# A chunked delta-rule layer: where projection units stand between the products of the triangular inversion's levels 1 to 5

## The reference, cut to what matters

```python
proj = x @ w_in
...
    k_beta = k * beta[..., None]
    a_mat = jnp.where(strict, jnp.einsum("bhncd,bhnsd->bhncs", k_beta, k) * decay, 0.0)
    rhs = jnp.concatenate([v * beta[..., None], k_beta * jnp.exp(gc)[..., None]], axis=-1)
    sol = lax.linalg.triangular_solve(a_mat, rhs, left_side=True, lower=True, unit_diagonal=True)
...
    def step(state, xs):
        u_c, w_c, qk_c, qd_c, kd_c, gl_c = xs
        v_new = u_c - jnp.einsum("bhcd,bhdv->bhcv", w_c, state)
        o_c = (jnp.einsum("bhcd,bhdv->bhcv", qd_c, state)
               + jnp.einsum("bhcs,bhsv->bhcv", qk_c, v_new))
        state = state * gl_c[..., None, None] + jnp.einsum("bhcd,bhcv->bhdv", kd_c, v_new)
        return state, o_c
```

## Time and profile before

| | |
|---|---|
| median of 3 runs | 2631.28 us (2630.43 to 2633.28) |
| the profiled execution's own time | 2627.11 us |
| its span, first to last instruction | 2625.5 us |
| PE busy over the span | 2399.2 us (91%) |
| DVE, ACT, POOL busy | 1760.8, 1331.4, 688.8 us |
| mean granted TensorE clock | 0.962 |
| the 16 solves | from about 200 to 1150 us of the span |

### The profile page before, as it was taken

How to read it: one execution, slowest core, us unless ns; L and a number is a source line. 1 busy time by engine, 2 the same in 40 slices (tenths; PEclk the granted TensorE clock), 3 DMA queues, 4 the chain that set the end, 5 groups by cost and what they waited for, 6 DMA issues and landing times. The chain is left out here.

```text
span 2625.5 us, 40683 instructions
## 1 busy us (share of the span) xinstructions
PE 2399.2 (91%) x11739; PEld 1957.8 (75%) x11740; DVE 1760.8 (67%) x2231; ACT 1331.4 (51%) x1735; POOL 688.8 (26%) x674
## 2 busy tenths in 40 slices
PE   7989988989999899967999887799999998999995
PEld 6868777877777788855787665688888887888782
DVE  3347888788778866645864585667767787677645
ACT  3254465456456544433531132567767776667640
POOL 2002121111221111104101222544444443444330
PEclk9989999999999999978999998899999999999997
DMA  3334432322233253335574234789999999899935
GB/s 116 74 45 72 62 49 58 87 65 49 65 65 64 54 91 99 93 112 185 156 232 174 96 97 153 251 276 341 291 289 299 321 327 346 283 285 297 330 78 214
DMA packets 244142, 435.92 MB, mean 166 GB/s; under 512 B 25096, under 2 KB 149000, under 8 KB 244046
## 3 DMA queue, kind: packets, MB, share of 16 engines
q1 hardware_dynamic: 211198, 350.70, 44.2%
q0 software_dynamic: 32848, 83.96, 12.3%
HBM read 370.88 MB, written 97.71 MB: 178 GB/s over the span
## 5 line engine op out<-in xcount | busy, mean ns | idle before, releaser
L59 PE MATMUL dn_pj<-x_hi,dn_hi 128*128 128x512 f32 x1024 | 433.9, 424 | 1.8 <-PEq L84 1.8
L61 PE MATMUL dn_pj<-x_hi,dn_lo 128*128 128x512 f32 x1024 | 406.6, 397 | 0.0
L60 PE MATMUL dn_pj<-x_lo,dn_hi 128*128 128x512 f32 x1024 | 405.0, 396 | 0.0
L1044 DVE SCALAR_TENSOR_TENSOR uc_half<-u_in,par,uc_half 128x512 f32<-128x512 f32 x480 | 378.4, 788 | 13.1
L59 PE MATMUL gu_ps<-e_hi,xg_hi 128*128 (+1 forms) x752 | 311.4, 414 | 0.0
L2520 DVE TENSOR_TENSOR e_lo<-e_raw,e_hi (+1 forms) x128 | 292.5, 2286 | 19.2 <-ACT e_hi L2459 19.0
L61 PE MATMUL gu_ps<-e_hi,xg_lo 128*128 (+1 forms) x752 | 295.7, 393 | 0.0
L60 PE MATMUL gu_ps<-e_lo,xg_hi 128*128 (+1 forms) x752 | 294.6, 392 | 0.0
L2459 ACT ACTIVATE e_hi<-e_raw (+1 forms) x128 | 245.1, 1917 | 42.4 <-PEq L84 35.5
L61 PEld LDWEIGHTS dn_pj<-x_hi,dn_lo 128*128 128x128 f32 x1024 | 195.7, 191 | 44.9
L59 PEld LDWEIGHTS dn_pj<-x_hi,dn_hi 128*128 128x128 f32 x1024 | 196.8, 192 | 33.7 <-issue 2.9
(11 more groups left out here) (388 smaller groups left out, 4966.1 us busy)
## 6 DMA issues: line engine op xcount, KB each, us to landing
e_raw<-in_w_gate_e_dram SPq DMA_DIRECT2D x128, 512.0 KB, 5.9
e_raw<-in_w_up_e_dram SPq DMA_DIRECT2D x128, 512.0 KB, 9.4
e_raw<-in_w_down_e_dram SPq DMA_DIRECT2D x128, 512.0 KB, 8.0
dn_raw<-in_w_in_dram SPq DMA_DIRECT2D x64, 512.0 KB, 7.9
gate_rows<-qkv_next SPq DMA_DIRECT2D x16, 512.0 KB, 3.1
br_raw<-in_w_oa_dram SPq DMA_DIRECT2D x16, 512.0 KB, 4.7
br_gate<-gate_rows SPq DMA_DIRECT2D x32, 256.0 KB, 4.6
br_raw<-in_w_ob_dram SPq DMA_DIRECT2D x16, 512.0 KB, 4.3
```

Of the source, the lines that this page charges most:

```text
L59: nc.tensor.matmul(out, w_hi, x_hi, start=first, stop=False)
L60: nc.tensor.matmul(out, w_hi, x_lo, start=False, stop=False)
L61: return nc.tensor.matmul(out, w_lo, x_hi, start=False, stop=last)
L1044: ins = stt(out=uc[:], in0=u_in[:, t:t + HALF], scalar=w, in1=uc[:], op0=ALU.mult, op1=ALU.add)
```

## The change

In levels 1 to 4 one unit stands behind Y, one behind T and one behind Z, where none, one and two stood before. In group 3, which has four units a level, it is one, one and two, where it was none, two and two. At level 5 the units that stood between T and Z (one, or two in group 3) stand between Y and T, and none is left between T and Z. Level 6 is as it was. The number of units is the same, and no other engine's list changes.

```diff
@@ -692,6 +692,7 @@
                                 last = mm(ga[:, pr, :], ar[l % NA][:, 2 * pr:2 * pr + 2, :].rearrange(FLAT),
                                           left_pair(xx, l, pr), start=True, stop=True)
                             last.then_inc(y_done, 1)
+                            f(1 if l < LEVELS - 2 or more else 2)
                             pe.wait_ge(xr_ready, q * 5 + l)
                             for pr in range(2):
                                 last = tr(gc[:, pr, :], xr[:, 2 * pr:2 * pr + 2, :].rearrange(FLAT), self.ident[:])
@@ -703,7 +704,10 @@
                             for u in range(4):
                                 last = mm(ga[:, u, 0:P // 2], atl[l % NA][:, u, :], left(xx, l, u), start=True, stop=True)
                             last.then_inc(y_done, 1)
-                        f(1 if more else 2)
+                        if l < LEVELS - 2:
+                            f(1)
+                        elif l == LEVELS - 1:
+                            f(1 if more else 2)
                         if more and p in (2, 3) and l <= 4:
                             if l == 1:
                                 pe.wait_ge(act_ln, 1 + q)
@@ -721,7 +725,7 @@
                                 last = mm(gb[0:P // 2, u, 0:P // 2], y6[:, u, :], xt[:, u, P // 2:P], start=True, stop=True)
                         last.then_inc(z_done, 1)
                         if l <= 4:
-                            f(2)
+                            f(1 if more else 2)
                         elif l == 5:
                             f(1 if more else 2)
```

## The result

The changed kernel took 2653.78 us (median of 4 runs, 2651.66 to 2657.50) against 2630.86 before: ratio 1.0095, 95% interval 1.0082 to 1.0107. A second comparison gave 1.0082 (1.0068 to 1.0096). So it is 0.8 to 1.0% slower: 22 and 25 us by the ratios, 22.6 and 22.9 by the medians, where 13.5 were forecast. The direction and the main places are those of the prediction, the size is not, and one term of it, the clock, was taken at nothing and is not.

The account below looks back on a forecast made before the run. PE together with the chain through ACT and DVE was taken to bound the solves. Losses of 0.7 to 1.9 us per solve summed to 13.5 us, clock 0, on the median 2631.3: 2644.8 us, range 2637 to 2655.

Parts of the forecast that it names:

- the clock: PE's stretches at 1.2 GHz over the solves: net cost taken as 0, possible from -4 to +10 us.
- The place and the mechanism: Level 5, T to Z: ACT's copy lies open, 0.91 us instead of 0.22, 0.69 lost in each of 16 solves.
- 1.9 us instead of 0.95: PE's wait before Y of level 4 at q = 8; the signs put it near 1.7 instead of 0.79.
- The gain of level 1: At q = 8 PE gets 1.16 us ahead at level 1, but DVE's list leaves Y of level 4 only 0.22 earlier.
- The sign at W: PE's idle time before W: up a quarter us or more in groups 0 to 2, the same in group 3.
- q = 1, 5, 9: 0.9 each: These three solves: Y of level 4 stays, level 5's copy comes 1.03 later, L960 had 0.1 to spare; 0.9 us lost each.
- The other solves: Losses per solve: 1.9 us at q = 0; 0.7 at q = 4, 8; 0.9 at 2, 6, 10; 0.7 at 3, 7, 11 and 12 to 15.
- rival 1: Added idle time near PE's waits brings 4 to 8 more low-clock stretches, +5 to +10 us, 2650 to 2655; chance 0.17.
- The floor of the prediction: Clock's lower bound: no stretch added, or three fall away at level 1 and level 3's T, -4 us.
- The price of one: One low-clock stretch behind PE's wait at T of level 3 costs about 1.28 us.
- Rival 2: Slack in DVE's list keeps 10 us won at level 1 and T of level 3 against 11 lost at level 5: 2632; chance 0.13.
- Rival 3: Faster: the same 10 us gain, level 5's copy hidden, T to Z costing under 0.3 us net: 2626; chance 0.05.

Follow-up runs that it names:

- e3_busy_waits: Changed kernel plus six unused matmuls in each of PE's waits before Y of level 4, T of level 3 and W, groups 0 to 2; 1.0035 of the kernel before.
- b3_busy: Kernel before plus unused matmuls in PE's waits, nine before T of level 3 and five before W, groups 0 to 2; 0.9955 of the kernel before.
- after_again: The changed kernel run once more, unaltered, for a second trace and more rounds; 1.0082 of the kernel before.
- e4_taps: Changed kernel with DVE's convolution taps shared out otherwise in groups 0 to 2, as many in all; 0.9941 of the kernel before.
- b4_level1_taps: b1_taps plus the units' new places at level 1 alone, levels 2 to 5 as in the kernel before; 0.9889 of the kernel before.
- b1_taps: Kernel before with only the shared-out DVE taps of e4_taps, units not moved; 0.9925 of the kernel before.

## Why the prediction was wrong in size

**The place and the mechanism: right.** Z of level 5 waits 16 times for ACT's copy; forecast were 0.91 us from T to Z, measured 0.94. No wait for `y_sb` is left at Z of level 1 that PE would notice in its groups. Y of level 4 waits 1.84 at q = 8 and 1.72 at q = 4. The prediction has two figures for it: "1.9 us instead of 0.95" in the working and "near 1.7 instead of 0.79" among the signs. The second is right: the row has 0.79, and 0.79 + 1.16 - 0.22 = 1.73. The gain of level 1 is swallowed by DVE's list: counted from the solve's start, Y of level 4 comes 0.21 earlier at q = 4 and 0.12 at q = 8 (0.23 and 0.22 in the second pair of traces); forecast was 0.22. The sign at W was missed in part: a quarter us more was forecast in groups 0 to 2, and it is 0.6 with p = 2 and 3, but 0.2 with p = 0 and 0.1 with p = 1.

**The term "q = 1, 5, 9: 0.9 each": too small.** Undisturbed, such a solve lost 1.42 us. The step that failed is "D of levels 2 to 5 are late by DVE's own list, which starts 0.14 later": the list also became longer. From D of level 1 to D of level 3 it was 12.88 us before (735.38 to 748.26) and 13.21 after (752.95 to 766.16), so Y of level 4 moved by 0.5 and not by 0.14. The reason is below, under what was not expected.

**The other solves: near.** Against the forecast of 1.9 (q = 0), 0.7 (p = 0), 0.9 (p = 2), 0.7 (p = 3) and 0.7 (group 3) undisturbed solves lost 2.1, 0.8, 1.0, 0.7 and 0.80. In group 3 this is the open chain alone: Z of level 5 came 0.73 later. All together, 2.1 + 2 x 0.8 + 3 x 1.42 + 3 x 1.0 + 3 x 0.7 + 4 x 0.8 = 16.3 us. The solves of e3_busy_waits and b3_busy, none of which met the low clock, say 16.5. The forecast was 13.5, so the chain was put 3 us too low, half of it at q = 1, 5 and 9.

**"I take 0" for the clock: wrong.** This is the larger failure, in size and in kind. The step was "the idle time is mostly in the same places and as long". It is not, and the prediction's own working had the longer wait before Y of level 4. From the first solve to the last, PE had 15 waits of over 1.5 us before and has 24 now: six before Y of level 4 (1.72 to 1.84 us, where it had been 0.79 with p = 0 and 0.2 with p = 1) and three before W with p = 3 (1.81, from 1.23) are new. In both pairs of traces the change added 10.2 us at 1.2 GHz, three stretches, by the rate 4.4 us. That is the mechanism of rival 1, just short of its 4 to 8 stretches and 5 to 10 us. The floor of the prediction, that stretches fall away at level 3's T because it waits 0.4 less, went the other way: there were four where there had been two. The price of one was near: 1.28 forecast, 1.5 on average, and 1.6 to 1.7 in a single solve of the changed kernel (33.70 us at q = 8 with one stretch, 32.01 in after_again with none).

**What is left.** 16.4 us of chain and 4.4 of clock are 20.8, and from Y of level 1 of the first solve to W of the last the traces differ by 21.0 us (21.6 in the second pair). Both comparisons have some 23 us by the medians and 22 and 25 by the ratios. The chance share of the clock between runs is as large as the rest, and I don't divide it further.

**Rivals 2 and 3.** Rival 2 fell because DVE's list had no slack: in e4_taps the wait of level 4 goes away with the taps alone. Rival 3 turned on T to Z at level 5 costing under 0.3 us more than 0.22, and it costs 0.72 more.

## What to carry to other kernels

Filling is worth something only where the engine would wait, and moving it opens the place that it leaves: a product whose operand makes a round trip through another engine (here 0.94 us from T to Z in place of 0.22) needs filling between, before any other place gets more. A gain ahead of an engine whose list is full is handed back at the next step that waits for that engine; look there first. b4_level1_taps is 1.1% faster than the kernel before, where the change alone lost 1%: 0.75% came from a fuller use of DVE's idle time (b1_taps) and the rest from the one part of the change that fills a real wait. And count a wait on PE of about 2 us at more than its length, for here some of them, not all, were followed by a stretch at 1.2 GHz that cost another 1.5 us.

## What was not expected of the hardware

**Matmuls nobody needs made the kernel faster.** In e3_busy_waits they took 16 us off the changed kernel by the ratios (1.0095 to 1.0035), and in b3_busy 12 us off the kernel before. From the first solve to the last the time at 1.2 GHz fell to 10.2 us in both, and all of that stands at the ends of the groups, at waits of 3.4 us into which nothing was put. Low stretches stood behind waits of 1.84 us (q = 8, above) and of 2.58 us (q = 2).

**DVE is slower while POOL works.** q = 9, DVE before:

```profile
735.72 5.04 DVE L1044 SCALAR_TENSOR_TENSOR uc_half<-u_in,par,uc_half 128x512 f32<-128x512 f32 x6
...
742.40 1.22 DVE L960 TENSOR_TENSOR dn_lo<-dn_raw,dn_hi 128x1024 fp32r<-128x1024 f32 x1
743.54 4.80 DVE L1044 SCALAR_TENSOR_TENSOR uc_half<-u_in,par,uc_half 128x512 f32<-128x512 f32 x5
```

and after:

```profile
753.29 5.17 DVE L1048 SCALAR_TENSOR_TENSOR uc_half<-u_in,par,uc_half 128x512 f32<-128x512 f32 x6
...
760.10 2.34 DVE L964 TENSOR_TENSOR dn_lo<-dn_raw,dn_hi 128x1024 fp32r<-128x1024 f32 x1
762.36 3.89 DVE L1048 SCALAR_TENSOR_TENSOR uc_half<-u_in,par,uc_half 128x512 f32<-128x512 f32 x5
```

POOL's mask of level 6 (`a_lvl`), released by Y of level 3, before:

```profile
743.83 1.60 POOL L1183 TENSOR_TENSOR a_lvl<-a_t,lvl_mask 128x512 f32<-128x512 f32 x1 [4.41 <-PE dn_a L692]
```

and after:

```profile
760.07 1.28 POOL L1187 TENSOR_TENSOR a_lvl<-a_t,lvl_mask 128x512 f32<-128x512 f32 x1 [4.52 <-PE dn_a L692]
```

Before, POOL's instruction fell on the taps, and five of them took 4.80 us in place of 3.89. After, Y of level 3 comes earlier in the solve, POOL starts 0.03 us ahead of L964, and that takes 2.34 in place of 1.22. That is 1.12 us more at L964 against 0.91 less at the five taps, 0.21 of the 0.33 by which the list grew; the six taps ahead (5.17 us for 5.04) are the rest. Over the whole trace after, L964 takes 1.22 us where no tensor instruction of POOL overlaps it (50 of 62). Where one does (12) it is one of two things: in eight POOL had started first and L964 took 2.31 to 2.37 us; in four L964 took its 1.22, and POOL's instruction took 2.29 to 2.37 in place of 1.28. So POOL's work is not free for DVE, and moving Y moved it onto a dearer instruction. The Trainium skill (SBUF — State Buffer, SBUF: two separate sides) says that a DVE instruction with two inputs in SBUF and a GpSimd instruction that reads SBUF lock each other out, and that the one that starts first has the ports for its whole instruction. The trace agrees in the main: the one that is longer is so by 1.0 to 1.2 us, close to the length of the other (1.28 and 1.22). In three of the eight POOL's instruction is longer too, 1.62 us; it had begun 0.4 us ahead, beside DVE's instruction before L964. In one of the four POOL's record begins 0.005 us ahead of L964, too little for its rough times to say who was first.
